# Even block of a two-layer diffusion backbone: the output projection in three fp32r passes instead of one fp32 pass

## What is computed

```python
yc, yl = even_mixer(hc @ ev_w_in[e], hl @ ev_w_in[e], ...)   # attention heads (512) | mLSTM heads (512)
w_out = ev_w_out[e]                                          # 1024 x 1024
x  = layer_norm(alpha * x  + gate(mod_l, 1) * (yl @ w_out), ln_g[l, 1], ln_b[l, 1])
cx = layer_norm(alpha * cx + gate(mod_c, 1) * (yc @ w_out), ln_g[l, 1], ln_b[l, 1])
```

## Time and profile before

| what | value |
|---|---|
| median of the three runs | 1960.8 us |
| the profiled execution's own time | 1961.69 us |
| its span, first to last instruction | 1960.0 us |
| busy: TensorE (PE) / VectorE (DVE) / ScalarE (ACT) / GpSimd (POOL) | 95% / 69% / 35% / 15% |
| mean granted TensorE clock | 0.967 of full speed |

### The profile page before, as it was taken

How to read it: one execution, slowest core, us unless ns; L and a number is a source line. 1 busy time by engine, 2 the same in 40 slices (tenths; PEclk the granted TensorE clock), 3 DMA queues, 4 the chain that set the end, 5 groups by cost and what they waited for, 6 DMA issues and landing times. The chain is left out here.

```text
span 1960.0 us, 25249 instructions
## 1 busy us (share of the span) xinstructions
PE 1862.0 (95%) x9616; PEld 1559.0 (80%) x9616; DVE 1354.9 (69%) x2331; ACT 692.2 (35%) x1143; POOL 301.9 (15%) x313
## 2 busy tenths in 40 slices
PE   6999999999997789899999999999999999989997
PEld 6888878898784455788887888888878898879997
DVE  7677777869975563877778357774687887564454
ACT  3222233345444431422224233222242543434443
POOL 0000001143000003400000232000044445140002
PEclk7999999999897899899999999999999999989999
DMA  9355444215431101454544233554234545405533
GB/s 360 129 195 204 171 188 166 98 56 138 151 147 59 44 1 43 165 201 171 207 152 174 102 123 122 211 193 153 107 111 169 214 175 204 170 3 186 198 150 111
DMA packets 43963, 290.17 MB, mean 148 GB/s; under 512 B 13916, under 2 KB 19676, under 8 KB 27232
## 3 DMA queue, kind: packets, MB, share of 16 engines
q1 hardware_dynamic: 35488, 271.13, 37.7%
q10 hardware_dynamic: 8384, 17.83, 2.4%
HBM read 272.16 MB, written 16.78 MB: 147 GB/s over the span
## 5 line engine op out<-in xcount | busy, mean ns | idle before, releaser
L1930 DVE CUSTOM_DVE_ANT_0 L<-slot 128x1024 f32<-128x1024 f32 x272 | 339.5, 1248 | 82.3 <-DMA slot<-in_ada_dram 75.1
L1277 ACT ACTIVATE w_hi<-slot 128x1024 fp32r<-128x1024 f32 x176 | 186.3, 1061 | 573.5 <-PE bank L681 558.2
L1979 DVE TENSOR_TENSOR w_lo<-slot,w_hi 128x1024 fp32r<-128x1024 f32 x176 | 216.8, 1234 | 204.4 <-ACT w_hi L1277 197.9
L676 PE MATMUL bank<-m_hi,w_hi 128*128 128x512 f32 (+1 forms) x1344 | 296.6, 363 | 3.2 <-ACT w_hi L1277 3.2
L681 PE MATMUL bank<-m_hi,w_lo 128*128 128x512 f32 (+1 forms) x1344 | 296.2, 363 | 0.1
L678 PE MATMUL bank<-m_lo,w_hi 128*128 128x512 f32 (+1 forms) x1344 | 296.1, 363 | 0.0
L676 PEld LDWEIGHTS bank<-m_hi,w_hi 128*128 128x128 f32 x1344 | 232.3, 189 | 43.1 <-ACT w_hi L1277 4.0
L681 PEld LDWEIGHTS bank<-m_hi,w_lo 128*128 128x128 f32 x1344 | 232.5, 189 | 39.7 <-DVE w_lo L1979 0.5
L678 PEld LDWEIGHTS bank<-m_lo,w_hi 128*128 128x128 f32 x1344 | 232.6, 189 | 39.3
L2160 DVE TENSOR_TENSOR down_lo<-slot,down_hi 128x1408 fp32r<-128x1408 f32 x64 | 108.8, 1716 | 116.1 <-ACT down_hi L1326 115.8
L739 PE MATMUL bank<-g_lo,down_hi 128*128 128x512 f32 (+1 forms) x770 | 154.7, 349 | 0.1
(11 more groups left out here) (393 smaller groups left out, 2929.8 us busy)
## 6 DMA issues: line engine op xcount, KB each, us to landing
slot<-in_gateup_dram SPq DMA_DIRECT2D x44, 2048.0 KB, 8.1
slot<-in_ada_dram SPq DMA_DIRECT2D x34, 2048.0 KB, 8.1
slot<-in_down_dram SPq DMA_DIRECT2D x32, 1408.0 KB, 6.4
slot<-in_ev_in_dram SPq DMA_DIRECT2D x4, 2048.0 KB, 8.8
slot<-in_od_in_dram SPq DMA_DIRECT2D x4, 2048.0 KB, 9.5
R<-s_ops SPq DMA_DIRECT2D x16, 512.0 KB, 5.7
s_tables<-slot ACTq DMA_DIRECT2D x8, 768.0 KB, 3.3
R<-s_tables SPq DMA_DIRECT2D x8, 768.0 KB, 6.7
```

The costliest lines, as they stand in the source:

```text
L676: nc.tensor.matmul(bank[j][:, c0:T], w_hi[:, off, c, :], m_hi[:, c, c0:T], start=(c == 0), stop=False)
L1277: nc.scalar.activation(w_hi[:, off, :, :].rearrange("p a b -> p (a b)"), slots[b][:, (2 * (f % 2) + off) * D:(2 * (f % 2) + off + 1) * D], ...
L1930: ins = nc.vector.tensor_tensor_reduce(out=junk, in0=slots[k][:, t * D:(t + 1) * D], in1=csilu[s_], scale=1.0, scalar=0.0, op0=ALU.mult, o ...
L1979: nc.vector.tensor_tensor(w_lo[b][:, t, :, :].rearrange("p a b -> p (a b)"), slots[b][:, t * D:(t + 1) * D], w_hi[:, off, :, :].bitcast(F3 ...
```

## The change

The even block gets an output projection of its own, `even_out_proj`, with three fp32r products per pair of tiles. It needs rounded parts and remainders of `y` and of `ev_w_out`: 16 ScalarE copies and 16 VectorE subtractions, set at given places in the two engines' lists. The remainders of `y` and of the weights are written in place over `y` and over slots 0 and 1. The rounded `y` lies in slot 2, the rounded weights of d = 0 to 3 in slot 3, those of d = 4 to 7 in `R`. The diff, cut to its core (`out_proj` stays for the odd block, without its even branches):

```diff
+OUT_HI = [("y", n) for n in range(4)] + [("w", n) for n in range(8)] + [("y", n) for n in range(4, 8)]
+OUT_LO = [("y", n) for n in range(4)] + [("w", n) for n in range(4)] + [("y", n) for n in range(4, 8)] + [("w", n) for n in range(4, 8)]
...
+        even_y_hi = rounded("even_y_hi", slots_at[2], 0, [P, KT, T])
+        out_hi = [rounded(f"out{d}_hi", *at, [P, KT, P]) for d, at in enumerate([(slots_at[3], 1024 * ((d + 1) % 4)) for d in range(4)] + [(R_at, 6144 + 1024 * d) for d in range(4)])]
...
+            def even_out_proj(between):
...
+                def inputs_rest(c):
+                    lo("y", c)
+                    for d in range(4):
+                        last = nc.tensor.matmul(proj_out(name, d)[:, :], out_hi[d][:, c, :], m_lo[:, c, :], start=False, stop=(c == KT - 1))
...
+                take(0)
+                for c in range(KT):
+                    hi("y", c)
+                    for d in range(4):
+                        if c == 0 and d == 2:
+                            pe.wait_ge(sem("ml_out_read"), 2 * HEADS)
+                        if c == 0:
+                            hi("w", d)
+                            lo("w", d)
+                        nc.tensor.matmul(proj_out(name, d)[:, :], out_hi[d][:, c, :], even_y_hi[:, c, :], start=(c == 0), stop=False)
+                        nc.tensor.matmul(proj_out(name, d)[:, :], w_lo[0][:, d, c, :], even_y_hi[:, c, :], start=False, stop=False)
+                    if c:
+                        inputs_rest(c - 1)
+                    if c == 2:
+                        between()
+                inputs_rest(KT - 1)
+                take(1)
+                for d in range(4, KT - 1):
+                    pe.wait_ge(sem("r_ready"), before("r_ready", name) + d - 3)
+                    hi("w", d)
...
+                    lo("w", d)
...
+                for s_ in range(2):
+                    a, b = STREAMS[s_]
...
ScalarE:
+                act.wait_ge(sem("na_probs_ready"), 2 * NA_PAIRS)
+                for c in range(4):
+                    out_inputs_hi(c)
...
                     exponentials(2 * hd)
                     if hd + 1 < HEADS:
                         queries_keys(hd + 1)
+                    if hd == HEADS - 1:
+                        act.wait_ge(used[3], slot_done[3])
+                        out_weights_hi(3)
                     exponentials(2 * hd + 1)
+                    if hd == 0:
+                        act.wait_ge(full[0], 16 * (uses_before("ffn1")[0]))
+                        for d in range(3):
+                            out_weights_hi(d)
                     if hd:
                         spreads(hd - 1)
+                act.wait_ge(full[1], 16 * (uses_before("ffn1")[1]))
+                act.wait_ge(sem("ml_scores_done"), HEADS)
+                act.wait_ge(sem("ml_out_done"), 2 * HEADS - 1)
+                for d in range(4, KT):
+                    out_weights_hi(d)
                 spreads(HEADS - 1)
...
+                for c in range(4, KT):
+                    out_inputs_hi(c)
                 squares("even", 0)
VectorE:
                 exponents(0)
+                for c in range(4):
+                    out_inputs_lo(c)
...
                             exponents(v + 1)
+                        for d in {1: (0,), 3: (1,), 7: (2, 3)}.get(v, ()):
+                            out_weights_lo(d)
                         quotients(v)
...
+                for c in range(4, KT):
+                    out_inputs_lo(c)
+                for d in range(4, KT):
+                    out_weights_lo(d)
                 out_residual(1, "even", (0, 1), 0)
```

More of the change, by code:

```diff
@@ L780, in norm_stats, with out_proj @@
                 nc.tensor.matmul(stat2_bank[:, a:b], mean_w[:, :], sq[:, (KT - 1) % 2, a:b], start=False, stop=True).then_inc(sem("stat"), 1)
-            def out_proj(name, slot_pair, c0, between=None):
+            def out_proj(name, slot_pair, c0):
                 take(slot_pair[0])
                 for c in range(KT):
-                    pe.wait_ge(sem(f"{name}_y{c // 4}"), c % 4 + 1 if c >= 4 or name == "odd" else 2 * (c + 1))
+                    pe.wait_ge(sem(f"{name}_y{c // 4}"), c % 4 + 1)
                     for d in range(4):
                         if c == 0 and d == 2:
-                            pe.wait_ge(*((sem("ml_out_read"), 2 * HEADS) if name == "even" else (sem("glu_read"), 4)))
+                            pe.wait_ge(sem("glu_read"), 4)
                         last = nc.tensor.matmul(proj_out(name, d)[:, c0:T], wslot(slot_pair[0])[:, d, c, :], y[:, c, c0:T],
@@ L793, in out_proj @@
                             last.then_inc(used[slot_pair[0]] if d == 3 else sem(f"{name}_out_done"), 1)
-                    if c == 2 and between:
-                        between()
                 take(slot_pair[1])
@@ L808, in out_proj @@
                                                 start=(c == 0), stop=(c == KT - 1))
-                        if c == 3 and s_ == 1 and name == "even":
+                    last.then_inc(used[slot_pair[1]] if s_ == 1 else sem("ctx_out_done"), 1)
+                norm_stats(name, 1)
+            def even_out_proj(between):
+                name = "even"
+                hi = lambda what, n: pe.wait_ge(sem("part_hi_ready"), EVEN_OUT_AT + OUT_HI.index((what, n)) + 1)
+                lo = lambda what, n: pe.wait_ge(sem("part_lo_ready"), EVEN_OUT_AT + OUT_LO.index((what, n)) + 1)
+                def inputs_rest(c):
+                    lo("y", c)
+                    for d in range(4):
+                        last = nc.tensor.matmul(proj_out(name, d)[:, :], out_hi[d][:, c, :], m_lo[:, c, :], start=False, stop=(c == KT - 1))
+                        if c == KT - 1:
+                            last.then_inc(used[0] if d == 3 else sem("even_out_done"), 1)
+                take(0)
[18 more added lines that the diff above has]
+                    hi("w", d)
+                    for c in range(KT):
+                        nc.tensor.matmul(proj_out(name, d)[:, :], out_hi[d][:, c, :], even_y_hi[:, c, :], start=(c == 0), stop=False)
+                    for c in range(KT):
+                        nc.tensor.matmul(proj_out(name, d)[:, :], out_hi[d][:, c, :], m_lo[:, c, :], start=False, stop=False)
+                    lo("w", d)
+                    for c in range(KT):
+                        last = nc.tensor.matmul(proj_out(name, d)[:, :], w_lo[1][:, d % 4, c, :], even_y_hi[:, c, :], start=False, stop=(c == KT - 1))
+                    last.then_inc(sem("even_out_done"), 1)
+                pe.wait_ge(sem("r_ready"), before("r_ready", name) + KT - 4)
+                hi("w", KT - 1)
+                lo("w", KT - 1)
+                for s_ in range(2):
+                    a, b = STREAMS[s_]
+                    for c in range(KT):
+                        nc.tensor.matmul(last_out(name, s_)[:, a:b], out_hi[KT - 1][:, c, :], even_y_hi[:, c, a:b], start=(c == 0), stop=False)
+                    for c in range(KT):
+                        nc.tensor.matmul(last_out(name, s_)[:, a:b], out_hi[KT - 1][:, c, :], m_lo[:, c, a:b], start=False, stop=False)
+                        last = nc.tensor.matmul(last_out(name, s_)[:, a:b], w_lo[1][:, 3, c, :], even_y_hi[:, c, a:b], start=False, stop=(c == KT - 1))
+                        if c == 3 and s_ == 1:
@@ L810, in out_proj @@
                             norm_stats(name, 0)
-                    last.then_inc(used[slot_pair[1]] if s_ == 1 else sem("ctx_out_done"), 1)
+                    last.then_inc(used[1] if s_ == 1 else sem("ctx_out_done"), 1)
                 norm_stats(name, 1)
@@ L1036, in turn_heads @@
                         last.then_inc(sem("ml_turned"), 1)
-                out_proj("even", (0, 1), 0, turn_heads)
+                even_out_proj(turn_heads)
             def head_means(name, c0):
```

15 lines of the change are left out of this document (14 added, 1 removed).

## The result

The changed kernel takes **1948.1 us** (median of four runs, 1947.04 to 1950.69) against 1960.7 for the kernel before: a ratio of 0.9935, 95% interval 0.9919 to 0.995. A second set of runs gave 1947.7 against 1961.3, 0.9928 [0.9913, 0.9944]; its 24 executions of the kernel before took 1956.0 to 1968.1 us. The forecast was 1952.6, with 1950.3 as its low end: the gain is 12.6 us where 8.2 were forecast. The profiled execution took 1950.69 us with a span of 1948.3, so the spans differ by 11.7; those of the second pair of profiles (1956.8 and 1946.4) differ by 10.4.

A forecast was written before the change was run, and what follows sets the result against it. TensorE, busy for 95% of the span, was taken to set the end up to d = 6, VectorE behind it; 1961.69 - 8.35 + 0.15 = 1953.5, against the median 1960.8 - 8.2 = 1952.6 us, range 1950.3 to 1956.0.

The forecast's parts named there:

- The price of a pair: Even output projection: three fp32r instructions of 0.2267 us make 0.680 us where fp32 took 0.858, saving 0.178 us per pair.
- TensorE's steps: TensorE's timeline through the even output projection, step by step: d = 7 starts at 765.4 instead of 773.75, 8.35 us earlier.
- The wait ahead of the second group: After the first 4 instructions TensorE waits for banks that `quotients(7)` reads: 1.21 us where 0.24 stood, costing 0.97.
- the one ahead of d = 4: A new small wait on VectorE's residual of d = 0: TensorE goes on at 749.05 instead of 748.6, 0.45 us.
- The losses that the prediction names: What reduces the at most 9.97 us from 56 pairs: 0.97, 0.45, and what the transposes wait for.
- the cover of d = 7 by VectorE: VectorE sets the pace at d = 7, so its matmuls, 5.8 us where fp32 took about 6.9, are worth nothing either way.
- ScalarE and VectorE: The new copies and remainders fit idle holes: weights 0 to 2 in 3.2 us, 0.9 us to spare before `quotients(7)`.
- The clock falls in the new wait: Rival, chance 0.15: the new 1.2 us gap in the projection halves TensorE's clock, costing 1.6 us, giving 1953.9 us.
- The next FFN's slow start ends sooner, or later: Rival, chance 0.12: the FFN's first dense matmuls at clock 0.50 shrink or grow, +-1.5 us, 1951.1 to 1954.1.
- The sum: Whole kernel: 1961.69 - 8.35 + 0.15 for small waits = 1953.5; against the median, 1960.8 - 8.2 = 1952.6 us.
- moves elsewhere: The next FFN's first load only comes earlier, other SyncE loads move with the last residual, and GpSimd sets nothing.
- a rule about the pace: Rival, chance 0.01: by the skill page's issue gap, 216 ns for 512 columns, the gain is 10.5 us, giving 1950.3.

The follow-up runs named there:

- VectorE late: The changed kernel with 16 idle, chained subtractions of 128x512 on VectorE ahead of the remainders of weights 4 to 7: 1957.1 us, 0.998.
- the filled kernel: The kernel before with twelve idle fp32r matmuls of 256 columns in TensorE's wait for GpSimd ahead of the odd block's last outputs: 1957.8 us, 0.9986.

## Why the prediction was right or wrong

- **The price of a pair, right.** 0.227 us per instruction, as the earlier trace rows had it.
- **TensorE's steps, right to 0.3 us.** The wait ahead of the second group was 1.02 us (forecast 1.21), the one ahead of d = 4 was 0.39 (0.45). c = 3 began at 734.26, which is 734.04 when the 0.22 us are taken off by which this trace is late at the projection's first matmul (734.1). d = 7 came 7.87 us earlier by the rows and 8.09 with these 0.22 us (8.35), in both pairs of traces. The series behind a break took 0.1 to 0.2 us more than their count times 0.2267, and the transposes' step 0.3 less. (The losses that the prediction names, 0.97, 0.45 and some 0.45 at the transposes, leave 8.1 of the 9.97; its steps, which it went by, give 8.35.) The lead at d = 7 was kept up to the next FFN (7.83 by the rows), so the cover of d = 7 by VectorE was as forecast.
- **ScalarE and VectorE, right.** Weights 0 to 2 took 2.96 us and ended at 678.44 (3.2 us; 678.5 to 679.4). The pair ahead of `quotients(7)` took 2.35 of its hole and left a wait of 1.07 (0.9). The last weights ended near 743.4 (744), 5 us ahead of the first residual.
- **"The clock falls in the new wait" did not come.** The granted clock was 1.00 from 724 to 766. The Trainium skill, TensorE: Matmul & The Clock Gate, section on HAM oscillation, warns that idle gaps throttle TensorE again. Behind the gap of 1.02 us the clock did not fall; behind one of 7.06 us, in the kernel with VectorE late, it was 0.50 (last section). By the same page's back-to-back gap a matmul of 512 columns would start every 216 ns; the rows here say 227.
- **"The next FFN's slow start ends sooner, or later", wrong in its premise.** The stretch at about half clock ended 12.8 us after the FFN's first matmul in before and 10.7 in after, so it did end sooner, yet the FFN took 251.3 and 251.5 us up to its down projection. The start of the FFN is set by VectorE, not by TensorE's clock, as a window of the kernel after shows (TensorE busy for 3.59 of 6 us, VectorE for 5.90):

```profile
780.00:786.00 6.00, 3.59 (x13) 2.78 (x12) 5.90 (x9) 2.94 (x7) 6.00 (x8) 0.50 1.00 381
```

- **The sum is the step that failed.** "1961.69 (the profiled execution) - 8.35 + 0.15 for small waits" lets everything behind d = 7 move by one amount. Up to the odd block it does. But the odd block and the last FFN then took 4.7 us less, by a load that landed 1.5 to 1.8 us sooner after its stage's start, a clock that stayed full through the rope matmuls (1.6 us), and shorter waits for down weights (1.9 us). The paragraph on moves elsewhere had put this term at nothing: it let the other loads move with the last residual, and gave no reason why they would land as before. Not one of the rivals looked beyond the next FFN, and the range's low end of 1950.3 came from a rule about the pace, which said nothing of this. In the profile of before, the three places could be seen: waits of 1.77 us on GpSimd and 1.28 us on ScalarE behind loads, and a window at 0.59 of the clock in a kernel whose mean is 0.967.
- **What stays open.** Why the table for the scan lands earlier in the changed kernel, and why the down weights do. The time at which the odd block starts does not decide the landing. With nine pairs left out the odd block starts as early as in the changed kernel, and the table lands late; with VectorE late it starts later than in before, and the table lands early. The landing goes with TensorE's list, one profile per kernel, by no mechanism that a run here isolates. The length of the wait alone does not decide the clock. The mean granted clock does not explain the gain either: it was 0.967 in the profile of before and 0.966 in that of after.
- **What is shown** is where the extra lies, and that the three passes alone do not bring it: the kernels with 18 and 35 idle matmuls have them too, and there the table lands as late as in before, with slow rope matmuls in one of the two. Nor does all of it need them: the kernel with nine pairs left out has none of them and a short last down projection, and the filled kernel has none and fast rope matmuls. It took 3 us less than before (1.0 to 4.5), of which its trace shows about half. For the early landing of the table this second part is not shown: no kernel made from before has it.

## What to carry to other kernels

Where a stage has its own timeline, a sum over its instructions and waits forecasts it to 0.3 us in eight; the same sum is no forecast for the whole kernel as long as other stages hang on loads that land just too late or on a clock at its edge. Look for such places anywhere in the profile of before (here a wait of 1.77 us that goes back to a DMA, with TensorE at half clock behind it), and let the range take in what they hold, in both directions. And measure a neutral edit beside the change: here a kernel with idle work at one place was 3 us faster (1.0 to 4.5), and by the medians the stages that an edit didn't touch took 1 to 6 us less in every edited kernel, part of which is scatter.

## What was not expected of the hardware

**A matmul of 32 columns cost nearly as much as one of 256, and the clock behind them fell.** 35 fp32r matmuls of 32 columns took 3.87 us, 0.11 us each, where 0.03 to 0.06 were expected (256 columns take 0.12, 512 take 0.227). Their weight loads, one for each, fill the window below (PEld, the second engine: 3.80 of 3.80 us for 35). That these set the pace is argued from this row alone. The eight of 512 columns behind them took 3.46 us, 0.43 each, though TensorE had been busy without a break. TensorE's timeline of that kernel, and its windows:

```profile
759.97 4.02 PE L852 MATMUL bank<-even_y_hi,out_hi 128*128 128x32 f32 x35
763.84 3.62 PE L854 MATMUL bank<-even_y_hi,out_hi 128*128 128x512 f32 x8
767.30 2.02 PE L856 MATMUL bank<-m_lo,out_hi 128*128 128x512 f32 x8
```

```profile
760.00:763.80 3.80, 3.80 (x36) 3.80 (x35) 0.88 (x2) 0.63 (x1) 3.16 (x3) 0.99 0.00 0
763.80:767.30 3.50, 3.50 (x11) 2.79 (x10) 0.00 (x0) 0.00 (x0) 0.00 (x0) 0.52 0.00 0
767.30:769.00 1.70, 1.70 (x9) 1.39 (x8) 0.00 (x0) 0.00 (x0) 0.00 (x0) 1.00 0.00 0
```

The granted clock went from 0.99 to 0.52, 2.4 to about 1.2 GHz, and back: a delay of 3.87 us cost 5.6 us between the projection's first matmul and d = 7.

**A wait of 7 us costs more than itself.** With VectorE late, TensorE's first matmuls behind the wait, and the window of the first eight:

```profile
756.00 3.75 PE L851 MATMUL bank<-even_y_hi,out_hi 128*128 128x512 f32 x8 [7.06 <-issue]
759.55 2.55 PE L853 MATMUL bank<-m_lo,out_hi 128*128 128x512 f32 x8
```

```profile
756.00:759.50 3.50, 3.50 (x8) 2.78 (x9) 2.25 (x6) 1.83 (x3) 3.37 (x4) 0.50 0.02 7
```

They start 3.55 us and 2.39 us ahead of the next eight, instead of 1.81: 2.3 us on top of the wait. Waits of 1.02, 1.21, 1.22 and 1.96 us left the clock at 1.00, while those of 1.34, 1.38, 1.73 and 1.77 in the odd block were followed by a clock of 0.52 to 0.59 over the next 3.6 us, and those of 2.76 and 2.98 by one of 0.50. No row here tells what makes the difference between 1.77 and 1.96.
